# Where the residual of a sub-layer gets into the accumulators: transposes on TensorE, or additions on VectorE and ScalarE

## The chip, the cores and the metric

One core of a Trainium2 chip runs the whole program in one launch. The metric is device microseconds of one execution; times are medians of several runs of the same kernel.

## The reference

A trunk of DEPTH = 2 layers over 256 tokens of 1024 columns, in float32. Each layer has three sub-layers, and each is wrapped in a norm with a residual, alpha = 4^(1/4):

```python
for l in range(DEPTH):
    x = _layer_norm(DN_ALPHA * x + 0.5 * _swiglu(x, ffn1_w_gate[l], ffn1_w_up[l], ffn1_w_down[l]), ln1_g[l], ln1_b[l])
    mix = _hybrid_mixer(x, ...)
    x = _layer_norm(DN_ALPHA * x + mix, ln2_g[l], ln2_b[l])
    x = _layer_norm(DN_ALPHA * x + 0.5 * _swiglu(x, ffn2_w_gate[l], ffn2_w_up[l], ffn2_w_down[l]), ln3_g[l], ln3_b[l])
```

`_layer_norm(x, g, b)` is `(x - mean) * rsqrt(var + eps) * g + b` along the columns. `_swiglu` is `(silu(x @ w_gate) * (x @ w_up)) @ w_down` with 2816 inner columns. The mixer projects x, runs three branches (latent attention, mLSTM, retention), gates each and ends in `@ w_out`.

## The kernel before, in words

**Numbers.** Every product is three float32r matmuls: the high and low parts of x (`xhi`, `xlo`, side by side in `xpair`) and of the weights (`whi`, `wlo`). Weights come through a ring of five slots of 128 x 2048 (a "unit", 1 MB). SP loads a unit into `raw` once the unit five before it is used (`w_used`), ScalarE makes `whi` (`hi`, line 547), VectorE makes `wlo` (`lo`, line 838), TensorE uses it. A layer is 33 units, 44 units and 33 units; 220 in all.

**Stages.** The five engines run their own instruction lists, written out by hand; semaphores order them. Stages 0 to 5 are the sub-layers, FFNs at 0, 2, 3, 5 and mixers at 1, 4. There are two tiles of 128 tokens.

**Accumulators.** The sum of the residual and the sub-layer stands token-major in PSUM banks 0 to 3, two banks for each tile of tokens. It is scaled by 1/alpha, so that the residual goes in as x itself. `seed` (line 1409) puts it there: x is kept feature-major in `xf`, and eight transposes of 128 x 128 on TensorE per tile write it. In an FFN `tile_half(t, u)` (line 1513) does four of them ahead of each of its four quarters of the first block of gate and up columns: it waits for `xf`, seeds, waits for the split x and does 12 matmuls (three passes of four). In a mixer the 16 transposes stand at the end, ahead of the first product with `w_out` (line 1887). The down products and the `w_out` products (`tokens`, line 1477) then add to the banks.

**The norm.** `last_rows` (line 1495) ends a stage: banks 0 and 1 first, then the rest of tile 1, with the turning of tile 0 between. VectorE's `layer_norm` (line 932) measures a bank each (`measure`, line 943), aggregates, takes 1/std from ScalarE's root, and writes normalised rows to `z`, the lower 512 columns itself (line 974), the upper by ScalarE (line 624). TensorE turns `z` back to feature-major (`turn_rows`, line 1400). VectorE and ScalarE apply gain and bias by feature on the way to `xf` (lines 926 and 609), and VectorE splits it (`split_x`, lines 912 and 914). Tile 1's turning waits for tile 0's to be read out. At stage 1 and 4 the first product is `mv`, with the same twelve-matmul quarters as an FFN but no seeds.

**The FFN behind that.** Block 0 is computed token-major and turned by four transposes (line 1568), split by `tile_split` (line 854); from block 1 on, gate and up are feature-major and the down product lags one block: line 1568 and the first down product both lie in the lap j = 1.

**The mixer.** VectorE and ScalarE take turns between weight splits and the branches' own work. In the last part, for each branch b and half h, come two gate units, one branch unit, sigmoids on ScalarE (line 800), and products and sums into `merged` on VectorE.

**Last norm.** Only the last one uses the gain and bias as rows (`g_row`, `b_row`, 512 KB each, the same row for all partitions). SP loads them after all weights.

The code touched, in part:

Of the kernel before, what the change touches and what calls it, by code (L numbers as in the profile page):

```python
# [13 lines left out]
P = 128  # L14
# [89 lines left out]
def build(nc, a):  # L104
# [17 lines left out]
    def sem(name):  # L122
        return ctx.enter_context(nc.semaphore(name))
# [11 lines left out]
    xhi, xlo = xpair[:, :, 0, :], xpair[:, :, 1, :]  # L135
    xf = sb("xf", [P, KC, SEQ])

# [18 lines left out]
    hlo = place("hlo", [P, 2 * SEQ], F32R, r_u2 + 6144)  # L156
    z = place("z", [P, TT, D_MODEL], F32, r_u2)
    hhi_last = place("hhi_last", [P, 2 * SEQ], F32R, r_u2 + 8192)
# [35 lines left out]
    q_rope = place("q_rope", [P, HEADS, SEQ], F32, r_y + 20480)  # L194
    g_row = place("g_row", [P, D_MODEL], F32, r_y)
    b_row = place("b_row", [P, D_MODEL], F32, r_y + 4096)

# [47 lines left out]
    gate_part, up_part, gate_summed, up_summed = sem("gate_part"), sem("up_part"), sem("gate_summed"), sem("up_summed")  # L245
    rows_loaded = sem("rows_loaded")
    y_bank = sem("y_bank")
    ln_stats, ln_var, ln_std = sem("ln_stats"), sem("ln_var"), sem("ln_std")
# [105 lines left out]
    def tile_no(stage, t):  # L354

        return stage * TT + t + 1

    def half_no(stage, t, half):

        return (stage * TT + t) * 2 + half + 1  # L360
# [34 lines left out]
    def _(sp):  # L395
# [16 lines left out]
        def chunks(src):  # L412
            return src.rearrange("(k p) n -> p k n", p=P)

        def load_in(l, m, lo, n):

            load(l * U_LAYER + MIX_BASE + m, chunks(a["w_in"][l, :, lo:lo + n]), (KC, n))
# [6 lines left out]
        def ffn(l, w):  # L424
            base = l * U_LAYER + FFN_BASE[w]
            wg, wu, wd = (a[f"ffn{w + 1}_w_{n}"] for n in ("gate", "up", "down"))

            def cols(src, f):
                return chunks(src[l, :, f * FB:(f + 1) * FB])

            def rows(f):
                return chunks(wd[l, f * FB:(f + 1) * FB, :])

            gate_up = cols(wg, 0), cols(wu, 0)
            for u in range(2):
                dst = unit(raw, base + u).rearrange("p (k c n) -> p k c n", k=KC // 2, c=2)
                if base + u >= RING:
                    sp.wait_ge(w_used, done_no(freed_by(base + u)))
                if l == w == 0:
                    for part, loaded in ((slice(0, 2), half_loaded[u]), (slice(2, 4), w_loaded[u])):  # L440
                        kks = slice(4 * u + part.start, 4 * u + part.stop)
                        for c, src in enumerate(gate_up):
                            sp.dma_start(dst[:, part, c, :], src[:, kks, :]).then_inc(loaded, 16)
                    if u == 0:
                        load_x(1)
                else:
                    for c, src in enumerate(gate_up):
                        sp.dma_start(dst[:, :, c, :], src[:, 4 * u:4 * u + 4, :]).then_inc(w_loaded[(base + u) % RING], 16)
            for j in range(1, NF):
                load(base + 3 * j - 1, cols(wg, j), (KC, FB))  # L450
                load(base + 3 * j, cols(wu, j), (KC, FB))
                load(base + 3 * j + 1, rows(j - 1), (2, D_MODEL))
            load(base + 3 * NF - 1, rows(NF - 1), (2, D_MODEL))

        def mixer(l):
# [16 lines left out]
            for m, c in ((12, C_RQ), (14, C_RK), (16, C_RV), (18, C_MO), (20, C_RG)):  # L472
                for i in range(2):
                    if c in (C_RV, C_MO, C_RG):
                        load_half(l, m + i, c, i)
                    else:
                        load_in(l, m + i, c + 256 * i, 256)
            for b in range(3):
                for h in range(2):
                    for i in range(2):  # L480
# [9 lines left out]

        sp.wait_ge(x_ready, half_no(3 * DEPTH - 1, 1, 1))
        for i, dst in enumerate((g_row, b_row)):
            sp.dma_start(dst[:, :], a["ln_rows"][DEPTH - 1, 2, i, :].partition_broadcast(P)).then_inc(rows_loaded, 16)
        for half in range(2 * TT):
# [45 lines left out]
    def _(act):  # L540
# [87 lines left out]
        def mixer(l):  # L628
# [158 lines left out]
            for b in range(3):  # L787
                turn = l * 3 + b
                for h in range(2):
                    for i in range(3):  # L790
# [8 lines left out]
                        for c in range(2):  # L799
                            last = act.activation(gate[:, 2 * i + c, :], ps[:, GATE_BANK[i], c * SEQ:(c + 1) * SEQ],  # L800
                                                  ACT.Sigmoid, bias=par_col(l, "gate_b", KC * b + 4 * h + 2 * i + c))
                        last.then_inc(gates_ready, 1)
            hi(m0 + 44)
            hi(m0 + 45)
# [29 lines left out]
    def _(dve):  # L834
# [5 lines left out]
        def ffn(l, w):  # L840
# [53 lines left out]
            lo(base + 3)  # L894
            tile_product(1)
            lo(base + 4)
            for j in range(1, NF):
                if j == 1:
                    tile_split()
                lo(base + 3 * j + 2)  # L900
                gate_sum(j)
# [6 lines left out]

        def split_x(stage, t, half):

            part, tok = slice(4 * half, 4 * half + 4), slice(t * P, (t + 1) * P)
            dve.tensor_copy(xhi[:, part, tok], xf[:, part, tok]).then_inc(x_hi, 1)
            dve.wait_ge(x_hi, half_no(stage, t, half))
            dve.tensor_tensor(xlo[:, part, tok], xf[:, part, tok], xhi[:, part, tok].bitcast(F32),
                              ALU.subtract).then_inc(x_ready, 1)

        def scale_x(stage, t):
# [14 lines left out]
        def layer_norm(l, w):  # L932
# [21 lines left out]
            def store_rows(t):  # L954

                dve.wait_ge(rows_loaded, 32)
                dve.wait_ge(ln_var, tile_no(turn, t))
# [32 lines left out]
            measure(2)  # L990
            dve.wait_ge(x_upper, tile_no(turn + 1, 0))
            split_x(turn + 1, 0, 1)
            measure(3)
            aggregate(1)
            invert(1)
            normalise(1)
            scale_x(turn + 1, 1)
            dve.wait_ge(x_upper, tile_no(turn + 1, 1))
            split_x(turn + 1, 1, 1)

        def mixer(l):
# [173 lines left out]
            lo(m0 + 2)  # L1175
            lo(m0 + 3)
            lo(m0 + 4)
            dve.memset(ml_v[:, :, :, DH:], 1.0).then_inc(ones_set, 1)
# [196 lines left out]
    def _(pe):  # L1375
# [132 lines left out]
        def ffn(l, w):  # L1508
# [4 lines left out]
            def tile_half(t, u):  # L1513

                out, kks, first = ps[:, TILE_BANK[t], :], range(4 * u, 4 * u + 4), 4 * u
                wh, wl = slot(base + u, 512)
                pe.wait_ge(x_upper if u else x_lower, tile_no(stage, t))
                seed(t, u)
                if stage == t == 0:
# [35 lines left out]
            for j in range(1, NF):  # L1555
# [28 lines left out]
                pe.wait_ge(w_lo, done_no(down))  # L1584
                pe.wait_ge(hid_lo, step_no(l, w, j - 1))
                pick = chunks_of(hhi, hlo)
                tile_rows(down, 0, pick)
                if j < NF - 1:
                    tile_rows(down, 1, pick).then_inc(w_used, 1)
# [4 lines left out]
        def mixer(l):  # L1594
# [90 lines left out]
            def head_turn(n):  # L1685

                pe.wait_ge(h_ready, l * 4 + (n + 1))
                for k in range(4):
                    last = pe.transpose(ps[:, BANK[f"hT{n}"], k * P:(k + 1) * P], hn[:, n, k * DH:(k + 1) * DH], ident)
                last.then_inc(h_turned, 1)  # L1690
# [153 lines left out]
            for b in range(3):  # L1844
                turn = l * 3 + b
                for h in range(2):
# [15 lines left out]
                    elif h:  # L1862
                        pe.wait_ge(branch_added, turn * 4 + 3)
                        pe.matmul(ps[:, BRANCH_BANK[0], 0:SEQ], ones, xf[:, 0, :], start=True, stop=True)
                    else:
# [15 lines left out]
            for i in range(MIX_OUT):  # L1881
# [3 lines left out]
                if i == 0:  # L1885
                    for t in range(TT):
                        seed(t, 0)
                        seed(t, 1)
                if i < MIX_OUT - 1:
# [70 lines left out]
```

## Time and profile before

| | |
|---|---|
| median of 3 runs | 1296.04 us (1295.96 to 1297.54) |
| the profiled execution, its own time | 1297.05 us |
| its span, first to last instruction | 1294.8 us |
| mean granted TensorE clock | 0.999 |
| TensorE matmul busy | 1280.5 us, 7985 matmuls |
| VectorE busy | 890.7 us |
| ScalarE busy | 638.3 us |
| queue of the weights (q1) | 231.78 MB, 56.0% of 16 DMA engines |

Busy time of TensorE is the union of modelled spans: two matmuls that follow each other overlap, so what one holds back is read from start to start, not from its duration. In a timeline several instructions of a kind are one row, with their count behind an x, and the time in brackets is idle time of that engine ahead of the row and what ended it.

### The profile page before, as it was taken

The page shows a single profiled execution, that of the slowest core. Times are in us where ns is not written, and L with a number is a line of the kernel's source. Part 1 is how long each engine was busy: PE and PEld are TensorE (multiplying, and loading weights), DVE is VectorE, ACT ScalarE, POOL GpSimd, SP SyncE. Part 2 cuts the span into 40 slices and gives each one's busy share as a digit, 9 for nine tenths or more (in the row PEclk, how much of TensorE's full clock was granted, in tenths as well). Part 3 has the DMA queues.
Part 4 walks back from the last instruction along what each step waited for, and adds up shares of the span by engine and source line. Part 5 has one row for each costly group of instructions (what it writes and reads, how often), then busy time and mean ns, then how long its engine had stood idle before and what let it go on. Part 6 is the DMA issues. An engine that isn't in the chain of part 4 may idle for free.

```text
span 1294.8 us, 18576 instructions
## 1 busy us (share of the span) xinstructions
PE 1280.5 (99%) x7985; PEld 1150.2 (89%) x7985; DVE 890.7 (69%) x1086; ACT 638.3 (49%) x654; POOL 71.2 (5%) x59
## 2 busy tenths in 40 slices
PE   8999999999999999999999999999999999999998
PEld 7888889998999988888888888899989998888886
DVE  6666667998675676665675666779976766766655
ACT  5444446684644444444454444456745443544441
POOL 0399000000000000000000000000000000000000
PEclk9999999999999999999999999999999999999999
DMA  8755547643566555555556655466436565655562
GB/s 295 234 187 188 193 147 223 185 130 102 193 194 196 171 181 180 186 193 195 173 185 195 195 190 190 140 196 196 131 99 199 191 196 163 192 187 188 187 192 95
DMA packets 176401, 234.80 MB, mean 181 GB/s; under 512 B 8064, under 2 KB 146944, under 8 KB 176192
## 3 DMA queue, kind: packets, MB, share of 16 engines
q1 hardware_dynamic: 175936, 231.78, 56.0%
q0 software_dynamic: 240, 1.71, 0.4%
q8 instruction: 63, 1.03, 0.3%
q10 hardware_dynamic: 144, 0.13, 0.1%
q14 instruction: 18, 0.15, 0.0%
HBM read 232.56 MB, written 1.05 MB: 180 GB/s over the span
## 4 chain that ended last, share of the span: by engine, by line
PE 97%; DVE 1%; DMA 1%; ACT 1%; issue 0%; DVEq 0%
PE ps L1477 22%; PE ps L1452 21%; PE ps L1460 11%; PE ps L1380 11%; PE ps L1379 11%; PE ps L1378 11%; PE ps L1443 5%; PE ps L1400 1%; PE ps L1412 1%; DMA raw<-w_in 1%; PE ps L1662 1%; PE ps L1621 0%; PE ps L1622 0%; ACT rot_sw L633 0%; PE ps L1648 0%; PE ps L1649 0%
## 5 line engine op out<-in xcount | busy, mean ns | idle before, releaser
L838 DVE TENSOR_TENSOR wlo<-raw,whi 128x2048 fp32r<-128x2048 f32 (+1 forms) x218 | 492.5, 2277 | 205.3 <-ACT whi L547 205.0
L547 ACT ACTIVATE whi<-raw 128x2048 fp32r<-128x2048 f32 (+1 forms) x218 | 413.3, 1898 | 282.9 <-DMA raw<-w_in 112.2
L1452 PE MATMUL ps<-xpair,whi 128*128 128x512 f32 x1216 | 290.0, 390 | 0.0
L1452 PEld LDWEIGHTS ps<-xpair,whi 128*128 128x128 f32 x1216 | 225.7, 188 | 45.3
L1378 PE MATMUL ps<-xpair,whi 128*128 128x256 f32 x800 | 224.1, 280 | 0.0
L1380 PE MATMUL ps<-xpair,wlo 128*128 128x256 f32 x800 | 222.5, 278 | 0.0
L1379 PE MATMUL ps<-xpair,whi 128*128 128x256 f32 x800 | 222.4, 278 | 0.0
L1460 PEld LDWEIGHTS ps<-xpair,wlo 128*128 128x128 f32 x1216 | 154.5, 189 | 6.1
L1460 PE MATMUL ps<-xpair,wlo 128*128 128x256 f32 x1216 | 156.4, 281 | 0.0
L1379 PEld LDWEIGHTS ps<-xpair,whi 128*128 128x128 f32 x800 | 150.5, 188 | 0.4
L1378 PEld LDWEIGHTS ps<-xpair,whi 128*128 128x128 f32 x800 | 150.1, 188 | 0.4
L1380 PEld LDWEIGHTS ps<-xpair,wlo 128*128 128x128 f32 x800 | 150.1, 188 | 0.0
L1477 PE MATMUL ps<-whi,hhi 128*128 128x512 f32 x320 | 125.0, 391 | 0.0
L1477 PE MATMUL ps<-wlo,hhi 128*128 128x512 f32 x320 | 125.0, 391 | 0.0
L1477 PE MATMUL ps<-whi,hlo 128*128 128x512 f32 x320 | 124.5, 389 | 0.0
L886 DVE CAST hhi<-hid 128x512 fp32r<-128x512 f32 x36 | 15.4, 427 | 113.2 <-PE ps L1477 113.2
L566 ACT ACTIVATE gsum<-ps 128x512 f32<-128x512 f32 x40 | 23.9, 598 | 137.8 <-PE ps L1460 137.8
L1477 PEld LDWEIGHTS ps<-whi,hlo 128*128 128x128 f32 x320 | 60.1, 188 | 12.8
L1477 PEld LDWEIGHTS ps<-whi,hhi 128*128 128x128 f32 x320 | 60.2, 188 | 11.5
L1477 PEld LDWEIGHTS ps<-wlo,hhi 128*128 128x128 f32 x320 | 60.2, 188 | 11.0
L1378 PE MATMUL ps<-yhi,whi 128*128 128x256 f32 x192 | 53.6, 279 | 0.0
L1379 PE MATMUL ps<-ylo,whi 128*128 128x256 f32 x192 | 53.1, 277 | 0.0
(234 smaller groups left out, 1598.7 us busy)
## 6 DMA issues: line engine op xcount, KB each, us to landing
raw<-w_in SPq DMA_DIRECT2D x60, 1024.0 KB, 5.2
raw<-ffn_w_down SPq DMA_DIRECT2D x44, 1024.0 KB, 4.9
raw<-ffn_w_gate SPq DMA_DIRECT2D x40, 1024.0 KB, 5.4
raw<-ffn_w_up SPq DMA_DIRECT2D x40, 1024.0 KB, 5.4
raw<-w_br SPq DMA_DIRECT2D x12, 1024.0 KB, 5.1
raw<-w_out SPq DMA_DIRECT2D x8, 1024.0 KB, 4.8
raw<-ffn_w_gate SPq DMA_DIRECT2D x6, 512.0 KB, 3.8
raw<-ffn_w_up SPq DMA_DIRECT2D x6, 512.0 KB, 4.7
```

The source lines that it names most:

```text
L547: act.activation(unit(whi, n), unit(raw, n), ACT.Copy).then_inc(w_hi, 1)
L566: act.activation(halves(gsum[:, :]), ps[:, FFN_GATE:FFN_GATE + 2, SEQ:], ACT.Copy).then_inc(gate_part, 1)
L838: dve.tensor_tensor(w_low(n), unit(raw, n), unit(whi, n).bitcast(F32), ALU.subtract).then_inc(w_lo, 1)
L886: dve.tensor_copy(dst_hi[:, :], hid[:, :]).then_inc(hid_hi, 1)
L1378: pe.matmul(out, w_hi_ap, x_hi_ap, start=start, stop=False)
L1379: pe.matmul(out, w_hi_ap, x_lo_ap, start=False, stop=False)
L1380: return pe.matmul(out, w_lo_ap, x_hi_ap, start=False, stop=stop)
L1400: last = pe.transpose(ps[:, 4 + k // 4, (k % 4) * P:(k % 4 + 1) * P], z[:, t, k * P:(k + 1) * P], ident)
L1443: last = pe.matmul(out, x[:, kk, t * P:(t + 1) * P], w[:, kk - first_kk, :], start=start and kk == x_kks[0], stop=stop and kk == x_kks[-1])
L1452: pe.matmul(ps[:, bank, :], wh[:, kk, cols], xpair[:, kk, :, :], start=kk == 0, stop=kk == KC - 1, skip_group_check=True)
L1460: last = pe.matmul(ps[:, bank, 0:SEQ], wl[:, kk, cols], xhi[:, kk, :], start=False, stop=kk == KC - 1, skip_group_check=True)
L1477: last = pe.matmul(ps[:, bank, :], x, w[:, kk, cols], start=start and i == 0, stop=stop and i == 2, skip_group_check=True)
```

## The change

`seed` is called in stage 0 only. Elsewhere the residual is written from `z`, which is still token-major, by an addition that has PSUM (FFN) or SBUF (mixer) as its output:

- The gain and bias rows of every norm are loaded, in the stream of weights: ahead of block 4 in an FFN, ahead of branch 2 in a mixer. `g_row` and `b_row` lie in another region, as does `z` (the one that `rq` and `rk` use later in a mixer).
- FFN: VectorE multiplies `z` by the gain row in place (`scale_row`), each tile after other work of block 0, and adds the bias row into banks 0 to 3 (`seed_ffn`) behind `tile_split`. TensorE waits for `seeded` before the first down product of either tile.
- Mixer: VectorE makes the same rows into `resid` (`keep_residual`), in the region of `xf`, behind the second `lo` of the mixer's own list. ScalarE copies them to the four banks after the gates of branch 1. TensorE waits for that before the first `w_out` product.
- `head_turn`'s four transposes of a bank carry a start flag on the first alone.
- In the norm, `measure(3)` and `aggregate(1)` come ahead of the split of tile 0's upper half, and that split's low part behind `normalise(1)`.

```diff
+        def load_rows(l, w):
+            for i, dst in enumerate((g_row, b_row)):
+                sp.dma_start(dst[:, :], a["ln_rows"][l, w, i, :].partition_broadcast(P)).then_inc(rows_loaded, 16)
...
             for j in range(1, NF):
+                if j == 4:
+                    load_rows(l, 2 * w)
...
             for b in range(3):
+                if b == 2:
+                    load_rows(l, 1)
...
-        sp.wait_ge(x_ready, half_no(3 * DEPTH - 1, 1, 1))
-        for i, dst in enumerate((g_row, b_row)):
-            sp.dma_start(dst[:, :], a["ln_rows"][DEPTH - 1, 2, i, :].partition_broadcast(P)).then_inc(rows_loaded, 16)
...
+                if b == 1:
+                    act.wait_ge(resid_ready, l + 1)
+                    act.wait_ge(y_lo, l * 6 + 6)
+                    for t in range(TT):
+                        for c in range(2):
+                            act.activation(ps[:, 2 * t + c, :], resid[:, t, 512 * c:512 * c + 512],
+                                           ACT.Copy).then_inc(seeded, 1)
...
             tile_product(1)
+            if nth:
+                scale_row(3 * l + 2 * w - 1, 0)
             lo(base + 4)
+            if nth:
+                scale_row(3 * l + 2 * w - 1, 1)
             for j in range(1, NF):
                 if j == 1:
                     tile_split()
+                    if nth:
+                        seed_ffn(3 * l + 2 * w - 1)
...
+        def scale_row(turn, t):
+            dve.wait_ge(rows_loaded, 32 * (turn + 1))
+            dve.tensor_tensor(z[:, t, :], z[:, t, :], g_row[:, :], ALU.mult).then_inc(gain_rows, 1)
+
+        def seed_ffn(turn):
+            for t in range(TT):
+                dve.wait_ge(gain_rows, tile_no(turn, t))
+                dve.tensor_tensor(ps[:, 2 * t:2 * t + 2, :], z[:, t, :].rearrange("p (a b) -> p a b", a=2),
+                                  b_row[:, :].rearrange("p (a b) -> p a b", a=2), ALU.add).then_inc(seeded, 1)
+
+        def keep_residual(turn):
+            for t in range(TT):
+                scale_row(turn, t)
+            for t in range(TT):
+                dve.wait_ge(gain_rows, tile_no(turn, t))
+                last = dve.tensor_tensor(resid[:, t, :], z[:, t, :], b_row[:, :], ALU.add)
+            last.then_inc(resid_ready, 1)
...
             measure(2)
-            dve.wait_ge(x_upper, tile_no(turn + 1, 0))
-            split_x(turn + 1, 0, 1)
             measure(3)
             aggregate(1)
+            dve.wait_ge(x_upper, tile_no(turn + 1, 0))
+            high_x(turn + 1, 0, 1)
             invert(1)
             normalise(1)
+            low_x(turn + 1, 0, 1)
...
             lo(m0 + 3)
+            keep_residual(3 * l)
             lo(m0 + 4)
...
-                pe.wait_ge(x_upper if u else x_lower, tile_no(stage, t))
-                seed(t, u)
+                if stage == 0:
+                    pe.wait_ge(x_upper if u else x_lower, tile_no(stage, t))
+                    seed(t, u)
...
+                if j == 1 and stage:
+                    pe.wait_ge(seeded, seeded_by(l, 2 * w) - 1)
                 tile_rows(down, 0, pick)
+                if j == 1 and stage:
+                    pe.wait_ge(seeded, seeded_by(l, 2 * w))
...
                 if i == 0:
-                    for t in range(TT):
-                        seed(t, 0)
-                        seed(t, 1)
+                    pe.wait_ge(seeded, seeded_by(l, 1))
```

## Rows read from the trace of the kernel before

**Rows 1.** The page: busy time of TensorE, and the granted clock in 40 slices.

```profile
PE 1280.5 (99%) x7985; PEld 1150.2 (89%) x7985; DVE 890.7 (69%) x1086; ACT 638.3 (49%) x654; POOL 71.2 (5%) x59
...
PEclk9999999999999999999999999999999999999999
```

**Rows 2.** The waits of TensorE: us in total, times, longest.

```profile
PE ps L1621 <- DVE q_rope L1020: 1.9, 2, 0.9
PE ps L1689 <- DVE hn L1146: 1.8, 1, 1.8
```

**Rows 3.** Groups by line, shapes apart: count | busy us, mean ns | idle before.

```profile
L1412 PE MATMUL ps<-cst,xf 128*128 128x128 f32 x96 | 13.8, 277 | 0.0
...
L566 ACT ACTIVATE gsum<-ps 128x512 f32<-128x512 f32 x40 | 23.9, 598 | 137.8 <-PE ps L1460 137.8
```

**Rows 4.** Timeline of TensorE, start of the FFN of stage 2.

```profile
465.51 0.60 PE L1412 MATMUL ps<-cst,xf 128*128 128x128 f32 x4
...
465.95 1.04 PE L1400 MATMUL ps<-cst,z 128*128 128x128 f32 x8
...
469.61 0.60 PE L1412 MATMUL ps<-cst,xf 128*128 128x128 f32 x4
469.96 2.10 PE L1443 MATMUL ps<-whi,xpair 128*128 128x512 f32 x8
...
472.82 0.60 PE L1412 MATMUL ps<-cst,xf 128*128 128x128 f32 x4
```

**Rows 5.** Timeline of TensorE, start of the mixer of stage 1.

```profile
198.16 1.06 PE L1400 MATMUL ps<-cst,z 128*128 128x128 f32 x8
...
200.90 1.99 PE L1443 MATMUL ps<-whi,xpair 128*128 128x512 f32 x8
...
203.63 1.98 PE L1443 MATMUL ps<-whi,xpair 128*128 128x512 f32 x8
```

**Rows 6.** Timeline of TensorE, where the first w_out product begins.

```profile
437.74 1.91 PE L1412 MATMUL ps<-cst,xf 128*128 128x128 f32 x16
...
439.40 0.48 PE L1477 MATMUL ps<-whi,mhi 128*128 128x512 f32 x1
```

**Rows 7.** Timeline of VectorE, norm ahead of stage 2: statistics of banks 2, 3, then z.

```profile
461.78 0.69 DVE L943 BATCH_NORM_STATS2 stats<-ps 128x6 f32<-128x512 f32 x1
...
463.44 0.69 DVE L943 BATCH_NORM_STATS2 stats<-ps 128x6 f32<-128x512 f32 x1
...
465.01 0.80 DVE L974 TENSOR_SCALAR z<-ps,mv,rstd 128x512 f32<-128x512 f32 x1
```

**Rows 8.** Timeline of VectorE, FFN of stage 2.

```profile
478.46 2.29 DVE L838 TENSOR_TENSOR wlo<-raw,whi 128x2048 fp32r<-128x2048 f32 x1 [1.38 <-ACT whi L547]
482.18 0.69 DVE L854 CAST hhi<-ps 128x512 fp32r<-128x512 f32 x1 [1.43 <-PE ps L1568]
482.91 0.69 DVE L856 TENSOR_TENSOR hlo<-ps,hhi 128x512 fp32r<-128x512 f32 x1
```

**Rows 9.** Timelines of TensorE and VectorE, the same FFN: down products, a pair of splits.

```profile
487.56 0.39 PE L1477 MATMUL ps<-whi,hhi 128*128 128x512 f32 x1
...
510.88 4.49 DVE L838 TENSOR_TENSOR wlo<-raw,whi 128x2048 fp32r<-128x2048 f32 x2
...
520.59 0.40 PE L1477 MATMUL ps<-whi,hhi 128*128 128x512 f32 x1
```

**Rows 10.** Timeline of VectorE, the third unit's split in both mixers.

```profile
212.85 2.06 DVE L838 TENSOR_TENSOR wlo<-raw,whi 128x1824 fp32r<-128x1824 f32 x1 [4.71 <-ACT whi L547]
...
851.03 2.06 DVE L838 TENSOR_TENSOR wlo<-raw,whi 128x1824 fp32r<-128x1824 f32 x1 [3.30 <-ACT whi L547]
```

**Rows 11.** ScalarE behind branch 1's gates; the loads (size each, us to landing).

```profile
411.25 1.92 ACT L547 ACTIVATE whi<-raw 128x2048 fp32r<-128x2048 f32 x1 [4.25 <-DMA raw<-w_in]
...
b_row<-ln_rows SPq DMA_DIRECT2D x1, 512.0 KB, 6.9
```

More of the change, by code:

```diff
@@ L135, in build @@
     xhi, xlo = xpair[:, :, 0, :], xpair[:, :, 1, :]
-    xf = sb("xf", [P, KC, SEQ])
+    r_xf = region(4 * KC * SEQ)
+    xf = place("xf", [P, KC, SEQ], F32, r_xf)
+    resid = place("resid", [P, TT, D_MODEL], F32, r_xf)
     r_rows, r_y, r_b, r_qk, r_rq, r_rk = (region(n) for n in (3072, 24576, 15360, 8192, 4096, 4096))
@@ L156, in build @@
     hlo = place("hlo", [P, 2 * SEQ], F32R, r_u2 + 6144)
-    z = place("z", [P, TT, D_MODEL], F32, r_u2)
+    z = place("z", [P, TT, D_MODEL], F32, r_rq)
     hhi_last = place("hhi_last", [P, 2 * SEQ], F32R, r_u2 + 8192)
@@ L194, in build @@
     q_rope = place("q_rope", [P, HEADS, SEQ], F32, r_y + 20480)
-    g_row = place("g_row", [P, D_MODEL], F32, r_y)
-    b_row = place("b_row", [P, D_MODEL], F32, r_y + 4096)
+    g_row = place("g_row", [P, D_MODEL], F32, r_b)
+    b_row = place("b_row", [P, D_MODEL], F32, r_b + 4096)
     k_rope = place("k_rope", [P, SEQ], F32, r_b)
@@ L246, in build @@
     rows_loaded = sem("rows_loaded")
+    gain_rows, seeded = sem("gain_rows"), sem("seeded")
+    resid_ready = sem("resid_ready")
     y_bank = sem("y_bank")
@@ L356, in tile_no, with seeded_by @@
         return stage * TT + t + 1
+    def seeded_by(l, w):
+        return 8 * l + (0, 4, 6)[w]
     def half_no(stage, t, half):
@@ L907, in ffn, with high_x, low_x @@
                     lo(base + 3 * j + 4)
-        def split_x(stage, t, half):
+        def high_x(stage, t, half):
             part, tok = slice(4 * half, 4 * half + 4), slice(t * P, (t + 1) * P)
             dve.tensor_copy(xhi[:, part, tok], xf[:, part, tok]).then_inc(x_hi, 1)
+        def low_x(stage, t, half):
+            part, tok = slice(4 * half, 4 * half + 4), slice(t * P, (t + 1) * P)
             dve.wait_ge(x_hi, half_no(stage, t, half))
@@ L915, in split_x @@
                               ALU.subtract).then_inc(x_ready, 1)
+        def split_x(stage, t, half):
+            high_x(stage, t, half)
+            low_x(stage, t, half)
+        def scale_row(turn, t):
[13 more added lines that the diff above has]
+            last.then_inc(resid_ready, 1)
         def scale_x(stage, t):
@@ L954, in store_rows @@
             def store_rows(t):
-                dve.wait_ge(rows_loaded, 32)
+                dve.wait_ge(rows_loaded, 32 * (turn + 1))
                 dve.wait_ge(ln_var, tile_no(turn, t))
@@ L1688, in head_turn @@
                 for k in range(4):
-                    last = pe.transpose(ps[:, BANK[f"hT{n}"], k * P:(k + 1) * P], hn[:, n, k * DH:(k + 1) * DH], ident)
+                    last = pe.matmul(ps[:, BANK[f"hT{n}"], k * P:(k + 1) * P], hn[:, n, k * DH:(k + 1) * DH], ident,
+                                     is_transpose=True, start=k == 0, stop=True, skip_group_check=True)
                 last.then_inc(h_turned, 1)
@@ L1863, in mixer @@
                         pe.wait_ge(branch_added, turn * 4 + 3)
-                        pe.matmul(ps[:, BRANCH_BANK[0], 0:SEQ], ones, xf[:, 0, :], start=True, stop=True)
+                        pe.matmul(ps[:, BRANCH_BANK[0], 0:SEQ], ones, resid[:, 0, 0:SEQ], start=True, stop=True)
                     else:
```

## The prediction

> **What bounds the kernel now.** I read the page's busy line first [rows 1]: TensorE is busy 1280.5 of 1294.8 us. The reader is to see that there are 14.3 us without a matmul in the whole run, so almost anything taken from TensorE's queue is taken from the time, and anything moved to VectorE or ScalarE is free until it makes TensorE wait. Next the list of waits, for TensorE alone [rows 2]: its waits after the start are a few of 1 to 2 us, on the rope and head-norm rows of VectorE in the mixer. None lies at the start of a sub-layer, where the change works. Then the group of the seeding transposes [rows 3], the timelines of TensorE where they stand [rows 4, 6] and of a place without them [rows 5], and last the gaps of VectorE, ScalarE and the load queue into which the new work is put [rows 7 to 11]. The granted clock stands at nine tenths or more in every slice [rows 1], its level of 2.4 GHz, so rows of one stage can be used for another.
>
> **What is removed: 80 transposes on TensorE.** `seed` stays in sub-layer 0 and goes in the five that follow a norm: 16 transposes in each of three FFNs, 16 in each of two mixers, 80 of the 96 in the group [rows 3]. The group's mean of 277 ns is the time that one is in the pipeline, not what it holds back: what counts is from start to start. In the FFN four seeds and the twelve matmuls behind them take from 469.61 to the next seeds at 472.82, 3.21 us [rows 4]. The mixer's first product is the same twelve matmuls with no seeds: 200.90 to 203.63, 2.73 us [rows 5]. Four seeds so cost 0.48 us: 0.35 from their start to the next matmul's (469.61 to 469.96) and 0.13 more in the slower first matmuls behind them. One group of the four stands ahead of the turning of the second tile, 465.51 to 469.61, 4.10 us [rows 4]. In the mixer the turning with eight matmuls takes 198.16 to 200.90, 2.74 us, and four more at 2.73/12 make 3.65; so 0.45 is saved there. An FFN saves 3 x 0.48 + 0.45 = 1.89 us, three save 5.67. In a mixer the 16 seeds stand together, 437.74 to 439.40, 1.66 us [rows 6]; with the same 0.13 behind them 1.79, two mixers 3.58. Sum 9.25 us, all of it on TensorE's path. Bounds: by the start-to-start times alone (0.35 and 1.66) it is 12 x 0.35 + 2 x 1.66 = 7.5; above it is 9.6, if the first group too counts with 0.48 and another 0.2 goes in small waits.
>
> The Trainium skill ("TensorE: Matmul & The Clock Gate", Part 4: PE-mode transpose) gives about 275 ns for a 128x128 transpose inside a kernel; by it the estimate would be 80 x 0.275 = 22.0 us. The trace has the same number as a duration and 0.11 us from start to start, so I do not use it for the sum.
>
> **Norm, new order on VectorE.** The second tile's statistics now come ahead of the split of the first tile's upper half, and the low part of that split behind the second tile's normalising. It matters because TensorE, rid of four seeds, wants the second tile's rows earlier: at 462.30 + 2.73 = 465.03 instead of 465.95 (462.30 is 465.51 less one period of 3.21) [rows 4]. In the old order the last statistics start at 463.44 and z is ready at 465.01 + 0.80 = 465.81, 2.37 us later [rows 7]. In the new one they can start as soon as the statistics of bank 2 end (461.78 + 0.69 = 462.47, at which the last product ends too), and the inserted cast costs about 0.1 net, since it lies under the wait for ScalarE's root. z is ready at 462.5 + 2.4 + 0.1 = 465.0. I take 0.09 us of new wait for each FFN, 0.27 in all. The ends are nothing and, if the reordering brought nothing, 465.81 - 465.03 = 0.8 each, 2.4 in all. At a mixer's start nothing is removed and the turning began one matmul's step behind the product before it [rows 5], so I count nothing.
>
> **New work on VectorE, FFN.** Tensor-tensor takes 0.69 us for 512 columns and 2.29 for 2048 [rows 8]; between them 1024 columns come to 0.69 + 0.53 = 1.22 us. `scale_row(0)` falls into the gap of 1.38 us before the split of a weight unit, `scale_row(1)` into the 1.43 us before `tile_split`, both waiting for TensorE or ScalarE [rows 8]. They cost nothing; without the cover up to 2.44. The two `seed_ffn` instructions stand behind `tile_split`, which ends at 482.91 + 0.69 = 483.60, and run to 486.04. TensorE takes bank 0 at 487.56 [rows 9] and bank 2 twelve matmuls (2.7 us) later, so the new wait on `seeded` is met by 2.7 us for the first tile (its seed is done at 484.8) and by 4.2 for the second, and both ends move together, since `tile_split` waits for TensorE itself. Writing PSUM from SBUF is in no row for this instruction; ends are 1.22 and twice that, at which the seeds would still land (486.0 and 488.5) before their use at 487.56 and 490.3. Behind the seeds are queued the next weight splits and the gate sum, 2.44 us late. A down unit's low part is ready at about 510.88 + 2.25 = 513.13 and used at 520.59: 7.4 us in hand in the steady state [rows 9], and every lap has over 2 us of idle on VectorE to recover. Cost nothing.
>
> **New work on VectorE and ScalarE, mixer.** `keep_residual` is four instructions of 1.22 us, less some overlap of about 0.08 each where they follow one another: 4.6 us, ahead of the split of the third unit. In layer 0 VectorE is idle 4.71 us just there, waiting for ScalarE, which waits for a load; in layer 1 it is idle 3.30 us [rows 10]. So nothing, and 1.3 us of delay to VectorE in layer 1, which the next idle stretches take up. If it were not covered: 1.3 us, or 4.6 per mixer if the gap itself moved. ScalarE's four copies of 512 columns at 0.6 us [rows 3] are 2.4 us, in the 4.25 us that it waits for a load after the last gate of branch 1 [rows 11]; they would be done by about 410, and TensorE's first output product starts at 439.40 [rows 6]. Cost nothing, without cover 2.4 each.
>
> **New loads on SP's queue.** Six loads of the norm's rows, 1 MB each, now stand in the stream of weights (the last one stood behind it). They wait for nothing; before unit `base + 11` in an FFN, before branch 2 in a mixer. The last pair landed 6.9 us after its issue [rows 11]. If nothing overlaps, the unit behind lands 6.9 us late, under the 7.4 us in hand [rows 9]; beside each other two transfers should overlap, so I expect 2 to 4. Cost nothing; it decides only above 7.4.
>
> **Sum.** 9.25 - 0.27 = 9.0 us. The profiled execution took 1297.05 us (span 1294.8 and 2.3 around it), so 1288.0 for it; it stands 1.0 above the median of 1296.04, to which the same difference is applied: 1287.0 us. The tail after the last product is not touched.
>
> **Rivals.**
> A. *The FFN's start becomes a wait.* TensorE arrives early and waits for the second tile's rows or their split. For it: it comes 0.9 us sooner to rows that were ready 0.14 us before they were used (465.81 against 465.95) [rows 4, 7]. Against it: the reordering, worked out above. It gives back up to the FFN's 5.67: 1287.0 + 5.7 = 1292.7.
> B. *The residual's work stands on the mixer's path.* VectorE would then delay the third unit by all of `keep_residual`, 2 x 4.6 = 9.2 us, and the change would be worth nothing: 1296.2. It needs the idle 4.71 and 3.30 us [rows 10] to move with the work; they hang on a load that does not change.
> C. *Slower: the row loads starve the ring.* One mechanism: each row load reads 4 KB for each of 128 partitions from the same source, in the queue ahead of weights. If beside the weights it holds them back 13.8 us, twice what it took alone, each of the six loads costs 13.8 - 7.4 = 6.4 us of wait, 38.4 together: 1287.0 + 38.4 = 1325.4. It makes the kernel slower than before from 7.4 + 9.0/6 = 8.9 us of delay on. Against it: 6.9 us measured [rows 11].
> D. *A transpose costs its whole duration.* 80 x 0.277 = 22.2 us: 1273.8. The starts 0.11 us apart (16 in 1.66) speak against it [rows 6].
>
> **How the numbers follow.** Forecast 0.81, A 0.08, B 0.05, C 0.04, D 0.02. What a measurement of this kernel can tell from no change is 0.2%, 2.6 us. Faster by more: forecast, A and D, 0.91; within: B, 0.05; slower: C, 0.04. The range: downward 9.6 us of gain and the 1.8 us of wait on head-norm rows that a shift could close [rows 2], 1284.6, taken as 1284.3; upward the 7.5 us end, 2.4 of waits at the norm and most of A, 1292.0.
>
> **What would show it.** Right: 16 seeds left in the group of `seed` in place of 96; twelve-matmul periods of 2.73 us between tile halves of an FFN; last branch product to first output product of a mixer with no gap; TensorE's busy time near 1271; no wait on `seeded`; the span 1285.8. The second tile's turning starts 3.6 us or less after the last accumulation. Wrong: in TensorE's waits a line on z or xpair of over 0.3 us per FFN (A), on wlo in the mixer's first units (B), on wlo or whi behind a row load (C). A span shorter by under 6 or over 11 us would say that the price of a transpose was read wrongly.

## The result, and the profile after

The changed kernel takes 1286.17 us, median of 6 runs (1286.02 to 1286.66); the kernel before, beside it, 1296.79 (1294.59 to 1299.46). The ratio is 0.9919, with the interval 0.9908 to 0.9930: faster by 10.6 us, where 9.0 was forecast (1287.0, range 1284.3 to 1292.0). The profiled execution took 1286.24 us, its span is 1283.9 (forecast 1285.8).

The page of the changed kernel, busy times and the loads of the norm's rows (last column: us from issue to landing):

```profile
PE 1272.0 (99%) x7905; PEld 1143.4 (89%) x7905; DVE 911.8 (71%) x1106; ACT 642.0 (50%) x662; POOL 68.8 (5%) x59
...
PEclk9999999999999999999999999999999999999999
...
q1 hardware_dynamic: 177376, 237.03, 57.5%
...
g_row<-ln_rows SPq DMA_DIRECT2D x6, 512.0 KB, 6.4
b_row<-ln_rows SPq DMA_DIRECT2D x6, 512.0 KB, 7.2
```

TensorE has 80 matmuls and 8.5 us of busy time fewer [rows 1]; VectorE has 21 us more and ScalarE 4 us more, and neither is anywhere near full. All waits of TensorE in the changed kernel:

```profile
PE ps L1466 <- DMA cst<-consts: 3.7, 1, 3.7
PE ps L1685 <- DVE q_rope L1078: 1.9, 2, 0.9
```

The reader is to see what is missing: no wait on `seeded`, on `z` or on `xpair`, and the 1.8 us on the head norm [rows 2] is gone too, which no part of the change touches. TensorE at the start of the FFN of stage 2, which answers to [rows 4]:

```profile
460.28 0.39 PE L1536 MATMUL ps<-whi,mlo 128*128 128x512 f32 x1
460.51 1.98 PE L1502 MATMUL ps<-whi,xpair 128*128 128x512 f32 x8
462.32 1.07 PE L1502 MATMUL ps<-wlo,xpair 128*128 128x512 f32 x4
463.23 1.04 PE L1459 MATMUL ps<-cst,z 128*128 128x128 f32 x8
464.02 2.09 PE L1502 MATMUL ps<-whi,xpair 128*128 128x512 f32 x8
...
466.86 1.98 PE L1502 MATMUL ps<-whi,xpair 128*128 128x512 f32 x8
...
469.58 1.98 PE L1502 MATMUL ps<-whi,xpair 128*128 128x512 f32 x8
```

From 466.86 to 469.58 is a period of 2.72 us, where 3.21 stood. The second tile's turning (L1459) follows the products before it with no wait. VectorE in the same place, then behind it (it answers to [rows 7, 8]):

```profile
459.99 1.42 DVE L1000 BATCH_NORM_STATS2 stats<-ps 128x6 f32<-128x512 f32 x2
...
462.29 0.81 DVE L1031 TENSOR_SCALAR z<-ps,mv,rstd 128x512 f32<-128x512 f32 x1
...
473.71 1.22 DVE L956 TENSOR_TENSOR z<-z,g_row 128x1024 f32<-128x1024 f32 x1
474.84 2.29 DVE L859 TENSOR_TENSOR wlo<-raw,whi 128x2048 fp32r<-128x2048 f32 x1
477.04 1.22 DVE L956 TENSOR_TENSOR z<-z,g_row 128x1024 f32<-128x1024 f32 x1
478.45 0.69 DVE L875 CAST hhi<-ps 128x512 fp32r<-128x512 f32 x1 [0.19 <-PE ps L1628]
479.17 0.69 DVE L877 TENSOR_TENSOR hlo<-ps,hhi 128x512 fp32r<-128x512 f32 x1
479.78 2.36 DVE L962 TENSOR_TENSOR ps<-z,b_row 128x1024 f32<-128x1024 f32 x2
```

The gaps of 1.38 and 1.43 us [rows 8] are used up: 0.19 is left of the second. The bias rows reach the banks (L962) at 482.14. TensorE's first down product comes at 483.82:

```profile
483.82 0.39 PE L1536 MATMUL ps<-whi,hhi 128*128 128x512 f32 x1
```

Both traces, set side by side by the end of each weight unit's last matmul, show where the time went. Each entry is how much the changed kernel is ahead at the end of the place less how much at its beginning:

| place | us gained |
|---|---|
| stage 0 and the first mixer up to its seeds | 0.02 |
| 16 seeds of the first mixer (0.02 to 1.79 ahead) | 1.77 |
| start of the FFN, stage 2 (1.79 to 3.74) | 1.95 |
| start of the FFN, stage 3 (3.72 to 5.66) | 1.94 |
| second mixer, head norm (5.74 to 7.09) | 1.35 |
| 16 seeds of the second mixer (7.10 to 8.86) | 1.76 |
| start of the FFN, stage 5 (8.89 to 10.83) | 1.94 |
| sum of these | 10.73 |

The span is 10.9 us shorter. The five places of the change make 9.36 of it, and 1.35 is the head-norm wait: the lead grows by 1.98 at the wait, of which 0.6 is given back in the units behind, where matmuls of 256 columns start 0.118 us apart in the changed kernel and 0.113 in the kernel before.

### The profile page after: what moved, and what is told of

It reads as the page before. It is cut to its first block, busy times and chain, and to the rows that moved or that the text cites. A ratio compares the mean times of both kernels' runs of the same rounds, so it can differ in the third digit from the quotient of the medians.

```text
span 1283.9 us, 18456 instructions
## 1 busy us (share of the span) xinstructions
PE 1272.0 (99%) x7905; PEld 1143.4 (89%) x7905; DVE 911.8 (71%) x1106; ACT 642.0 (50%) x662; POOL 68.8 (5%) x59
## 4 chain that ended last, share of the span: by engine, by line
PE 98%; DVE 1%; ACT 1%; DMA 0%; DVEq 0%; issue 0%
PE ps L1536 22%; PE ps L1511 22%; PE ps L1519 11%; PE ps L1439 11%; PE ps L1437 11%; PE ps L1438 11%; PE ps L1502 5%; PE ps L1459 1%; PE ps L1726 1%; PE ps L1685 0%; PE ps L1686 0%; ACT rot_sw L647 0%; PE ps L1712 0%; PE ps L1713 0%; PE ps L1711 0%; PE ps L1727 0%
```

## Experiments

Twelve experiments follow. Medians of the kernel before, run beside them, were 1296.54 (E1 to E4), 1296.48 (E5 to E8), 1295.70 (E9 to E11) and 1295.89 (E12).

**E1. The FFN part undone.** The changed kernel, with `seed` back in every FFN, without `scale_row` and `seed_ffn` there.

```diff
-                if stage == 0:
-                    pe.wait_ge(x_upper if u else x_lower, tile_no(stage, t))
-                    seed(t, u)
+                pe.wait_ge(x_upper if u else x_lower, tile_no(stage, t))
+                seed(t, u)
...
-                    if nth:
-                        seed_ffn(3 * l + 2 * w - 1)
```

> The changed kernel with its FFN part undone: the 48 transposes of the three FFNs are back on TensorE, VectorE's gain and bias work there is gone, the mixers stay changed. My theory (a group of four seeds holds TensorE back 0.48 us, start to start): 5.7 to 5.9 us over the changed kernel's 1286.2, so 1292.0. Rival D (0.277 us each): 13.3 us over, 1299.5. Rival A (the FFN's gain comes back as waits): within 1 us of 1286.2.

Measured: 1292.50 (1292.18 to 1292.54), ratio to before 0.9964 (0.9951 to 0.9977). That is 6.3 over the changed kernel: the FFN part is worth 6.3, a little over what was expected.

**E2. The mixer part undone.** `seed` back ahead of the first `w_out` product, without `keep_residual` and ScalarE's copies.

```diff
                 if i == 0:
-                    pe.wait_ge(seeded, seeded_by(l, 1))
+                    for t in range(TT):
+                        seed(t, 0)
+                        seed(t, 1)
...
-            keep_residual(3 * l)
```

> The changed kernel with its mixer part undone: the 32 transposes ahead of the w_out products are back, keep_residual and ScalarE's four copies are gone. My theory: 1.66 us of starts and 0.1 of settling per mixer, 3.4 to 3.6 us over 1286.2, so 1289.7. Rival B (the residual's work stands on the mixer's path): the undoing costs nothing or gains. If the two undone parts together give less than the 10.6 us between the two kernels, by over 1 us, there is a third part: a wait on the head-norm rows in layer 1 that the trace of before has and the trace of after lacks.

Measured: 1289.94 (1289.44 to 1292.13), ratio 0.9948 (0.9935 to 0.9962), 3.8 over the changed kernel. The two parts add up: 6.3 + 3.8 = 10.1 of 10.6. Each is on TensorE's path, and neither leans on the other.

**E3. The old order of the norm in the changed kernel.**

```diff
-            measure(3)
-            aggregate(1)
             dve.wait_ge(x_upper, tile_no(turn + 1, 0))
-            high_x(turn + 1, 0, 1)
+            split_x(turn + 1, 0, 1)
+            measure(3)
+            aggregate(1)
             invert(1)
             normalise(1)
-            low_x(turn + 1, 0, 1)
```

> The changed kernel with the norm in its old order on VectorE. My theory: z of the second tile is ready 0.8 us after TensorE wants to turn it, in each of three FFNs, and nothing at the mixers: 2.1 to 2.4 us over 1286.2, so 1288.4, with waits of TensorE on z in the trace. Rival (the order is of no account): 1286.2.

Measured: 1289.05 (1288.84 to 1289.57), ratio 0.9939 (0.9926 to 0.9951), 2.9 over the changed kernel. Its waits of TensorE show which wait it is:

```profile
PE ps L1458 <- DVE z L1031: 2.1, 3, 0.7
```

Three waits of 0.7 us, one for each FFN and none for a mixer. By units the three places lose 0.92, 0.87 and 0.92: more than the wait, since what follows it is slower too. Rival A was real, and it is the new order that keeps it away.

**E4. Every seed twice in the kernel before.** 96 more transposes.

```diff
-            for k in range(4 * half, 4 * half + 4):
+            for k in 2 * list(range(4 * half, 4 * half + 4)):
                 pe.matmul(ps[:, 2 * t + half,
```

> The kernel before with every seeding transpose issued twice, 96 more. It is the price of a transpose by itself. My theory: 0.109 us each from start to start, 92 of them exposed (the first four of stage 0 stand where TensorE waits anyway): 10.0 us over before, ratio 1.0077. Rival D (0.277 us): 26 us, ratio 1.020.

Measured: 1305.64 (1304.79 to 1305.71), ratio 1.0064 (1.0051 to 1.0077): 9.1 over the median of before, 10.0 over the 1295.6 around which its lower executions lie (E12). A transpose behind others so costs TensorE 10.0 / 96 = 0.104 us (0.095 by the median). The trace agrees without any median: a period of four seeds and twelve matmuls, now with eight seeds, goes from 472.85 to 476.46, 3.61 us in place of 3.21, so 0.100 for each of the four added, and the 16 added ahead of `w_out` take 1.75 us, 0.109 each:

```profile
472.85 1.03 PE L1412 MATMUL ps<-cst,xf 128*128 128x128 f32 x8
...
476.46 1.03 PE L1412 MATMUL ps<-cst,xf 128*128 128x128 f32 x8
```

The duration of a transpose in the same trace is still 0.27:

```profile
L1412 PE MATMUL ps<-cst,xf 128*128 128x128 f32 x192 | 24.0, 273 | 0.1
```

Rival D (0.277 each, 26 us here) is refuted.

**E5. Before, the head norm ahead of a weight split.** It takes the wait away that the change took away in passing.

```diff
-            lo(m0 + 25)
             head_norm(1)
+            lo(m0 + 25)
```

> The kernel before, with one pair swapped in VectorE's list of the mixer: the second head norm (head_norm(1)) ahead of the weight split lo(m0 + 25), which waits for a load. In the trace of before TensorE waits 1.8 us for these rows in layer 1, behind a load that landed after 7.3 us where its twin in layer 0 took 5.2. Theory (this wait comes and goes with the load, and makes part of the 10.6 us and of the spread of before): 1 to 2 us under before, and a spread of runs under 1 us. Rival (a chance of one profile): same as before within 0.5 us.

Measured: 1295.66 (1295.39 to 1296.19, 12 runs), ratio 0.9992 (0.9984 to 1.0000); the head-norm wait is gone, and the profile has another one, of 0.8 us, at the start (see E12). The median falls by 0.8 only, but the spread is 0.8 us where the runs of before beside it have 5.7 (1294.73 to 1300.45).

**E6. Stage 0 as well.** The changed kernel, with three of the four banks of stage 0 filled by copies on VectorE and only four seeds left; in place of the warm-up transposes at the start, TensorE writes the three banks once with a start flag, so that the products behind accumulate.

```diff
+                    else:
+                        dve.tensor_copy(ps[:, 1, :], z[:, 0, 512:]).then_inc(seeded, 1)
+                        dve.tensor_copy(ps[:, 2:4, :], z[:, 1, :].rearrange("p (a b) -> p a b", a=2)).then_inc(seeded, 1)
...
-                if stage == 0:
-                    pe.wait_ge(x_upper if u else x_lower, tile_no(stage, t))
+                if stage == t == u == 0:
+                    pe.wait_ge(x_lower, tile_no(stage, t))
                     seed(t, u)
```

> The changed kernel carried on to stage 0: only the first four seeds stay on TensorE, banks 1 to 3 get x from VectorE (two copies from z behind tile_split). The flags of these banks are set by transposes of the identity in the place of the idle-time transposes at the start. Theory: three groups of 0.48 us, less two or three 0.1 us for the longer start: 1.2 to 1.5 us under 1286.2, so 1284.9. Rival (stage 0 hangs on loads and splits, the wait moves): 1286.2.

Measured: 1285.86 (1285.59 to 1288.27, 6 runs), ratio 0.9923 (0.9909 to 0.9936): 0.3 better than the changed kernel, where 1.2 to 1.5 was expected, and not to be told from it. The profiled execution is the one of 1288.27. It gains 0.8 us in stage 0, by units, and loses more in the second mixer. One stretch in the changed kernel and then in this one (columns: busy time and count of TensorE, weight loads, VectorE, ScalarE, GpSimd, then the granted clock):

```profile
1000.00:1040.00 40.00, 40.00 (x354) 39.95 (x352) 25.14 (x24) 16.11 (x17) 0.00 (x0) 1.00 0.67 211
```

```profile
1000.00:1040.00 40.00, 40.00 (x342) 40.00 (x341) 24.46 (x24) 16.15 (x17) 0.00 (x0) 1.00 0.64 210
```

Both are full, at the same granted clock, and the second does 342 matmuls where the first does 354. What sets the pace is open.

**E7. More work at `keep_residual`.** In the changed kernel each of its two additions made three times, with a wait for the one before; `again` is a new semaphore.

```diff
+                for n in range(2):
+                    dve.tensor_tensor(resid[:, t, :], z[:, t, :], b_row[:, :], ALU.add).then_inc(again, 1)
+                    dve.wait_ge(again, turn // 3 * 4 + 2 * t + n + 1)
                 last = dve.tensor_tensor(resid[:, t, :], z[:, t, :], b_row[:, :], ALU.add)
```

> The changed kernel with each addition of keep_residual done three times: four more instructions, some 5.0 us of VectorE ahead of the split of the mixer's third unit, in both layers. In the trace of after that split ends 3.0 us before TensorE takes the unit (214.4 against 217.5, and 848.5 against 851.5). Theory (cover, then a wait for what is over): 5.0 - 3.0 = 2.0 us per layer, and VectorE's next idle 2.5 us take up what follows: 4 us over 1286.2, so 1290.2. Rival B (all of it on the path): 10 us over. Rival (cover is larger than the rows say): 1286.2.

Measured: 1294.62 (1293.29 to 1296.01, 12 runs), ratio 0.9982 (0.9973 to 0.9991): 8.4 over the changed kernel, for 2 x 5 us of work and twice what was expected. The profiled execution is the quickest, 7.1 over. Its waits of TensorE, and the first of the two on its timeline:

```profile
PE ps L1441 <- DVE ml_v L1244: 5.3, 2, 2.6
```

```profile
220.16 0.36 PE L1441 MATMUL ps<-xpair,whi 128*128 128x256 f32 x1 [2.62 <-DVE ml_v L1244]
...
222.24 0.41 PE L1441 MATMUL ps<-xpair,whi 128*128 128x256 f32 x1
222.45 0.41 PE L1442 MATMUL ps<-xpair,whi 128*128 128x256 f32 x1
```

TensorE waits for the copies of v that stand behind the next weight split on VectorE, not for the split that the prediction watched. And the wait is not all: from 222.03 on matmuls of 256 columns start 0.21 us apart, before it 0.12. The windows of this kernel:

```profile
205.00:215.00 10.00, 10.00 (x82) 9.81 (x81) 9.90 (x9) 4.21 (x4) 0.00 (x0) 1.00 1.04 293
215.00:222.00 7.00, 4.38 (x36) 4.21 (x35) 6.97 (x7) 5.68 (x5) 0.00 (x0) 0.98 0.99 307
222.00:230.00 8.00, 8.00 (x59) 8.00 (x58) 7.90 (x9) 2.32 (x7) 0.00 (x0) 0.81 0.16 38
```

Behind the wait the granted clock falls to 0.81 in the stretch (the trace's record has it at the lower of its two levels, 1.2 in place of 2.4 GHz, from 221.70 to 225.11), and the first mixer loses 4.4 us in all, by units. In the second mixer the same wait costs 2.9 and the clock stays up.

**E8. Four times the row loads.** In the changed kernel three more pairs of rows loaded in each FFN, into room of their own, behind the first pair.

```diff
+                for c in range(3):
+                    for i in range(2):
+                        sp.dma_start(spare[:, c, i, :], a["ln_rows"][l, w, i, :].partition_broadcast(P)).then_inc(more_loaded, 16)
```

> The changed kernel with three more loads of the same rows (1 MB each, into spare memory) behind the row loads of the FFNs of stages 2, 3 and 5. In the trace of after one such load made the next unit's high part wait 4.2 us where it waits 2.8 otherwise. Theory (transfers overlap and run at the rate at which two units in flight run, some 3 us for 1 MB): the unit is 9 us later still, against 10.7 in hand, so 0 to 1 us per FFN: 1286.2 to 1289. Rival C (6.9 us each, nothing overlaps): 21 us later, over 10 us of wait in each of three FFNs, 1316 or more.

Measured: 1286.43 (1286.07 to 1288.42, 6 runs), ratio 0.9926 (0.9912 to 0.9940), 0.3 over the changed kernel. The unit behind the loads on ScalarE, in the changed kernel and then in this one; the changed kernel's next such unit, with no row load ahead of it, stands second:

```profile
507.17 1.92 ACT L561 ACTIVATE whi<-raw 128x2048 fp32r<-128x2048 f32 x1 [4.23 <-DMA raw<-ffn_w_gate]
...
522.45 1.92 ACT L561 ACTIVATE whi<-raw 128x2048 fp32r<-128x2048 f32 x1 [2.99 <-DMA raw<-ffn_w_gate]
```

```profile
514.79 1.92 ACT L569 ACTIVATE whi<-raw 128x2048 fp32r<-128x2048 f32 x1 [11.94 <-DMA raw<-ffn_w_gate]
```

One pair delays the unit by 4.23 - 2.99 = 1.2 us, four pairs by 9.0, and TensorE waits for neither. Even in this kernel the unit's high part is done at 514.79 + 1.92 = 516.71, and TensorE takes the unit 5.5 us later:

```profile
522.23 3.79 PE L1524 MATMUL ps<-xpair,whi 128*128 128x512 f32 x16
```

Rival C is refuted, its threshold too: the unit behind the rows has 9.0 + 5.5 = 14.5 us in hand.

**E9. The head norm's swap in the changed kernel** (the edit of E5).

> The changed kernel with head_norm(1) ahead of lo(m0 + 25) on VectorE in the mixer, the same swap that took VectorE's head-norm wait away from the kernel before. Theory: in the changed kernel TensorE has no wait on the head norm any more in its profiled execution, so the swap has nothing to take away: 1286.2, between 1285.8 and 1286.6, and the spread of the runs stays under 1 us. Rival: the head-norm wait is only hidden in the execution that was profiled and costs up to 1.8 us in others; then the median falls by 0.5 to 1.8, to 1284.4 to 1285.7. Second rival: the swap delays the split of unit 25 and costs: over 1286.6.

Measured: 1286.67 (1286.32 to 1286.99), ratio 0.9929 (0.9915 to 0.9943). There was nothing left to take away. The interval overlaps the changed kernel's, so whether the swap costs 0.5 isn't settled; by units its profiled execution is within 0.2 us of the changed kernel's all the way.

**E10. Less work more at `keep_residual`.** As E7, but each addition made twice.

```diff
-                for n in range(2):
+                for n in range(1):
```

> The changed kernel with each of the two additions of keep_residual made twice, so 2 instructions more in each mixer, with a wait for the first one to finish, together about 2.5 to 2.9 us on VectorE at the place; with four more the run grew by 8.4 us. Theory (cover with an edge): the changed kernel has about 2.4 us in hand in front of the copies of v, since four additions made waits of 2.6 us; two additions are just covered, so the time grows by 0 to 1 us, 1286.2 to 1287.2, with a wait of at most 0.5 us on v_copied. Rival B (no cover, VectorE's work there is on the path): half of the 8.4, 4.2 us, 1290.4. Third: the loss comes mainly from the clock, which falls after any wait of TensorE there; then a wait of some tenths already costs over 1.5 us.

Measured: 1287.03 (1286.57 to 1287.76), ratio 0.9934 (0.9920 to 0.9948), 0.9 over the changed kernel. VectorE comes to the copies of v 2.4 us later than in the changed kernel:

```profile
214.96 0.68 DVE L1240 COPY ml_v<-ps 128x512 f32<-128x512 f32 x1
```

```profile
217.34 0.68 DVE L1244 COPY ml_v<-ps 128x512 f32<-128x512 f32 x1
```

TensorE loses 0.34 and 0.31 us at the two places, by units, in a gap too short for the list of waits, and the clock stays. So the changed kernel has 2.4 - 0.3 = 2.1 us in hand there. By that E7, whose split of the third unit starts 5.0 us later (217.35 against 212.38), should lose 2.9 at each place, and its two starts stand 2.9 apart (217.26 to 220.16). The cover has an edge: E10 lies on it, and half of E7's 8.4 is not what half its work costs.

**E11. Both extra edits** (those of E6 and E5) in the changed kernel.

> The changed kernel with both extra edits: three of the four banks of stage 0 filled by VectorE copies in place of 12 transposes, and head_norm(1) ahead of lo(m0 + 25). Theory: the first alone gave 0.3 us (1285.86) and the second takes nothing or up to 0.5: 1285.2 to 1285.9. Rival: the copies' 12 transposes are worth 1.2 us as they were elsewhere, and were hidden by the slow executions of the earlier run: 1284.6 to 1285.1.

Measured: 1286.03 (1285.52 to 1286.20), ratio 0.9923 (0.9910 to 0.9936). Its profiled execution gains 1.0 us in stage 0 by units, yet the median lies 0.1 under the changed kernel's. No version tried beats it by more than can be measured.

**E12. The kernel before, unchanged, once more.**

> The kernel before, unchanged, profiled a second time. Theory: the wait of 1.8 us on the head norm of the second layer is not a fixed cost of the kernel before but hangs on when one w_in load lands, so it is there in some executions only. Then an execution near the lowest times (1295 to 1296) has no such line in the waits of TensorE, and one at 1297 or more has it; the median is 1295.5 to 1297 and the runs again lie 1.5 us or more apart. Rival: the wait is in every execution of the kernel before, and then it shows again whatever the time, and the change removes it by its timing (1.8 of the gain of 10.6 us); the spread would have another cause.

Measured: 1295.92 (1295.05 to 1298.80, 12 runs). Seven runs lie between 1295.05 and 1295.94 (middle one 1295.61), five between 1297.13 and 1298.80. The profiled execution is the one of 1298.80. Its waits of TensorE, without the load of constants and the rope rows:

```profile
PE ps L1443 <- ACT whi L811: 0.8, 1, 0.8
PE ps L1689 <- DVE hn L1146: 0.8, 1, 0.8
```

The head-norm wait is 0.8 here, 1.8 in the first profile [rows 2], and E4's profile, with the same order on every engine, has none. It goes with the load in front of it. In the first profile ScalarE waited 7.25 us for that load, here 6.23, in E4 5.06 (and 5.03 in the changed kernel, which has no head-norm wait either):

```profile
983.66 1.92 ACT L547 ACTIVATE whi<-raw 128x2048 fp32r<-128x2048 f32 x1 [7.25 <-DMA raw<-w_in]
```

```profile
984.77 1.92 ACT L547 ACTIVATE whi<-raw 128x2048 fp32r<-128x2048 f32 x1 [6.23 <-DMA raw<-w_in]
```

But this execution, though slower than the first profiled one (1297.05), has the shorter head-norm wait. Its loss is at the start:

```profile
9.31 2.07 PE L1443 MATMUL ps<-whi,xpair 128*128 128x512 f32 x4 [0.79 <-ACT whi L811]
11.18 1.05 PE L1443 MATMUL ps<-wlo,xpair 128*128 128x512 f32 x2
12.04 1.53 PE L1443 MATMUL ps<-whi,xpair 128*128 128x512 f32 x4
```

The matmuls of 512 columns start 0.43 us apart, in place of 0.23 elsewhere, and the first unit ends 2.2 us later than in the first profile. It isn't the wait that slows them. E5's profile has the same wait, and full pace behind it:

```profile
9.03 1.19 PE L1443 MATMUL ps<-whi,xpair 128*128 128x512 f32 x4 [0.81 <-ACT whi L811]
```

What differs is how long the slow pace of the start lasts. In every profile the first transposes start 0.213 us apart, about twice the later distance, and in E12 they still do ahead of the wait. The trace's record of the granted clock has full speed from 6.5 us on in E4, 7.5 in E5, 8.0 in the first profile, 9.0 in the changed kernel and only 13.0 in E12. Ahead of that there is no record, and the clock column shows 1.00 there, so that the column hides it and the starts show it. The Trainium skill ("TensorE: Matmul & The Clock Gate", "Wait — 56ns, not 53.3ns?") gives 426.7 ns from start to start for 512 columns at the lower clock; by that figure this is the lower level. Why it lasted longer in this execution is open.

The theory of one cause for the spread fell: the two profiles of the kernel before differ at the start and at the head norm. The rival (head-norm wait in every execution) isn't refuted: both profiles of this kernel have the wait, and E4, which lacks it, is another kernel. What the two losses make of the whole spread isn't shown; E5's twelve runs, with the same start and no head-norm wait, stay within 0.8 us.

## Why the prediction was right

**The main term.** The 80 seeds were priced at 9.25 us from start-to-start times. By units they gave 1.77 + 1.76 in the mixers (1.79 each) and 1.95 + 1.94 + 1.94 in the FFNs (1.89 each): 9.36. E1 and E2 put the shares at 6.3 and 3.8. Reading the starts and not the 277 ns of [rows 3] decided it: the figure of about 275 ns in the Trainium skill ("TensorE: Matmul & The Clock Gate", Part 4) is a duration by this trace, and E4 measures what a transpose holds back as 0.104 us. With the slower first matmuls behind a group, 9.36 / 80 = 0.117. The span is 10.9 us shorter, close to the 11 from which on the prediction would have called this price misread; what lies over the five places is the head norm's and not the price's.

**The norm.** 0.09 us of new wait for each FFN was taken; the trace has none: VectorE's half of `z` for the second tile is ready at 462.29 + 0.81 = 463.10, and TensorE wants it at 463.23. The bound without the new order, 0.8 each, was measured as three waits of 0.7 (E3), though the time went up by 2.9 and not 2.4.

**VectorE's and ScalarE's new work.** Forecast and measured: 1.22 and 1.22 us for each `scale_row`, 2.44 and 2.36 for the two `seed_ffn`, which end 1.7 us before the first down product (the second tile's bank is due another 2.7 later, so 4.4 in hand, 4.2 forecast). `keep_residual` takes 4.54 us (4.6), from 207.84 to 212.38:

```profile
207.84 2.35 DVE L956 TENSOR_TENSOR z<-z,g_row 128x1024 f32<-128x1024 f32 x2
210.11 2.35 DVE L971 TENSOR_TENSOR resid<-z,b_row 128x1024 f32<-128x1024 f32 x2
212.38 2.05 DVE L859 TENSOR_TENSOR wlo<-raw,whi 128x1824 fp32r<-128x1824 f32 x1
```

The split of the third unit starts without idle time before it, at 212.38 where it started at 212.85 [rows 10]: the idle 4.71 us has been filled, as forecast, and rival B's gap did not move. ScalarE's copies (2.4 forecast) lie where they were put:

```profile
406.82 2.14 ACT L822 ACTIVATE ps<-resid 128x512 f32<-128x512 f32 x4
411.55 1.92 ACT L561 ACTIVATE whi<-raw 128x2048 fp32r<-128x2048 f32 x1 [2.59 <-DMA raw<-w_in]
```

What the prediction missed here is where the cover ends. It named the unit's `wlo` as the first to be late; E7 and E10 show that it is the copies of v, with 2.1 us in hand, and that past the edge the price can be more than the wait.

**The loads.** 2 to 4 us of delay were expected and 1.2 found. The threshold was wrong too: by 7.4 us in hand [rows 9], E8's 9.0 us of delay should have cost 1.6 us in each of three FFNs, 4.8 together, and 0.3 was measured, with no wait. The 7.4 us were read at a down unit's low part [rows 9], not at the gate unit that stands behind the rows; that one has 14.5 us in hand by E8.

**The 1.6 us beyond the forecast.** The sum stood against a median of before that isn't its quickest. Against the lower seven of E12 (1295.61) the changed kernel gains 9.4, the sum of its five places. The rest is in what before's executions lose in some runs and the changed kernel's six did not: the head-norm wait, 1.35 us net in the profiled pair, which the prediction named only for the lower end of its range, and the start. That the change closes the head-norm wait by its timing isn't shown; none of the changed kernel's variants has it in its profile, but E4 hasn't either. This wait was no term of the sum. The changed kernel's own profile reaches full clock 1.0 us later than the first profile of before, and its six runs lie within 0.6 us; why none of them has a start as slow as E12's, when its first stage is the same code, is open.

## What to carry to other kernels

Price an operation on the bounding engine by the distance of starts with and without it in the same stretch, not by its duration: here 0.12 against 0.28 us. Work moved to an engine with idle time is free as far as the first consumer behind it allows, and that consumer is found by doubling the moved work, not by looking at the next instruction. When a queue feeding a bounding engine gets shorter by 0.5 us, look for the producer that was just in time, and move its chain forward in the same edit (here 2.9 us of 10.6).

## What the runs showed of the hardware that was not expected

- Behind a wait of TensorE of 2.6 us the granted clock fell to 0.81 in the next 8 us of E7's first mixer and stayed at 1.00 behind the same wait in the second.
- The slow pace of the start ends at another time in each execution: full clock is on record from 6.5 us (E4) to 13.0 us (E12) after the first instruction. Until then the clock column shows 1.00, while E12's matmuls of 512 columns start 0.43 us apart.
- At a granted clock of 1.00 and TensorE full, matmuls of 256 columns have two paces, 0.113 and 0.118 us apart; one profile can have the first and the next the second for the same stretch of work (E6: 342 matmuls in 40 us, 354 in the changed kernel; the two profiles of the kernel before part by 0.6 us over some 140 matmuls behind the head norm).
- Four pairs of row loads (1 MB for a pair, each row 4 KB at its source and read for 128 partitions) held the next weight unit back by 9.0 us, one pair by 1.2.
